# Order of the seven products of a feed-forward pair: the continuation of the first bank moves from third to fifth place

## What is computed

```python
h = rmsnorm(x, norm_ffn_pre[i])
gate, up = jnp.split(h @ ffn_w_gate_up[i], 2, axis=-1)
x = x + rmsnorm((jax.nn.silu(gate) * up) @ ffn_w_down[i], norm_ffn_post[i])
```

## Time and profile before

| | us |
|---|---|
| median of 3 runs | 3061.6 |
| lowest and highest | 3060.26, 3063.1 |
| profiled execution, its own time | 3064.46 |
| its span, first to last instruction | 3062.6 |
| the 20 pairs in it, first to last product | 705.9 to 950.3 |

### The profile page before, as it was taken

How to read it: one execution, slowest core, us unless ns; L and a number is a source line. 1 busy time by engine, 2 the same in 40 slices (tenths; PEclk the granted TensorE clock), 3 DMA queues, 4 the chain that set the end, 5 groups by cost and what they waited for, 6 DMA issues and landing times. The chain is left out here.

```text
span 3062.6 us, 43424 instructions
## 1 busy us (share of the span) xinstructions
PE 2715.5 (89%) x16618; PEld 1653.0 (54%) x16619; DVE 1141.4 (37%) x2326; ACT 654.9 (21%) x1327; POOL 312.2 (10%) x389
## 2 busy tenths in 40 slices
PE   7999999999999998999977999989788993898755
PEld 3445556578885484557554545445544642454323
DVE  2430157437889932227152111011422624232114
ACT  3440148421100010108131000000221621010002
POOL 0000012004441000000001100000100001122100
PEclk9999989999999999999988999999899996899887
DMA  5223120119545641120027889999632015999994
GB/s 201 83 83 101 53 97 29 59 56 259 198 161 199 259 181 59 55 90 1 28 75 296 346 352 412 397 413 382 256 126 89 1 63 204 370 364 377 404 418 170
DMA packets 137313, 594.52 MB, mean 194 GB/s; under 512 B 20336, under 2 KB 40588, under 8 KB 90608
## 3 DMA queue, kind: packets, MB, share of 16 engines
q1 hardware_dynamic: 86704, 359.25, 31.0%
q10 hardware_dynamic: 41808, 212.75, 17.3%
q0 software_dynamic: 8688, 21.00, 1.9%
HBM read 574.06 MB, written 33.69 MB: 198 GB/s over the span
## 5 line engine op out<-in xcount | busy, mean ns | idle before, releaser
L159 PE MATMUL psum<-normed,weight_ring 128*128 128x512 f32 (+1 forms) x896 | 365.2, 568 | 12.3 <-PEq L174 7.6
L159 PEld LDWEIGHTS psum<-normed,weight_ring 128*128 128x128 f32 x896 | 171.6, 192 | 201.4 <-issue 198.2
L1203 DVE SCALAR_TENSOR_TENSOR psum<-weight_ring,condition_rows 128x1024 f32<-128x1024 f32 x192 | 267.7, 1394 | 16.0 <-issue 0.9
L159 PE MATMUL psum<-modulated,weight_ring 128*128 128x384 f32 (+2 forms) x640 | 228.7, 518 | 0.0
L2469 PE MATMUL psum<-weight_ring,slot_rows_turned 128*32 128x256 f32 x2176 | 143.5, 409 | 73.3 <-DMA weight_ring<-in_w_dram 46.8
L2622 DVE COPY expert_hidden_turned<-psum 128x128 f32<-128x128 f32 (+1 forms) x93 | 32.7, 352 | 466.9 <-PE psum L2480 466.9
L2458 PE MATMUL psum<-weight_ring,slot_rows_turned 128*64 128x256 f32 x1792 | 205.3, 382 | 0.6 <-issue 0.6
L159 PEld LDWEIGHTS psum<-modulated,weight_ring 128*128 128x128 f32 x640 | 121.4, 190 | 105.5 <-issue 51.0
L2458 PEld LDWEIGHTS psum<-weight_ring,slot_rows_turned 128*64 128x64 f32 x1792 | 127.5, 138 | 76.0 <-issue 16.8
L2487 PE MATMUL psum<-weight_ring,expert_hidden_turned 128*32 128x256 f32 (+1 forms) x1536 | 168.0, 445 | 0.0
L2550 ACT ACTIVATE expert_silu<-psum 64x256 f32<-64x256 f32 (+1 forms) x91 | 34.6, 380 | 604.6 <-PE psum L2458 322.6
(11 more groups left out here) (444 smaller groups left out, 3791.7 us busy)
## 6 DMA issues: line engine op xcount, KB each, us to landing
third_stream_weights<-in_w_dram ACTq DMA_DIRECT2D x93, 2048.0 KB, 14.2
weight_ring<-in_w_dram SPq DMA_DIRECT2D x84, 2048.0 KB, 17.1
weight_ring<-in_w_ada_dram SPq DMA_DIRECT2D x24, 2048.0 KB, 8.9
weight_ring<-in_w_ffn_dram SPq DMA_DIRECT2D x11, 2048.0 KB, 12.8
weight_ring<-in_w_rnn_dram SPq DMA_DIRECT2D x8, 1536.0 KB, 11.8
weight_ring<-in_w_att_dram SPq DMA_DIRECT2D x6, 2048.0 KB, 8.0
weight_ring<-in_w_in_dram SPq DMA_DIRECT2D x6, 2048.0 KB, 12.8
weight_ring<-in_w_down_dram SPq DMA_DIRECT2D x8, 1408.0 KB, 6.4
```

The source lines that it names most:

```text
L159: last = nc.tensor.matmul(out, weights[:, k * P:(k + 1) * P], rhs(k), start=(k == 0), stop=(k == tiles - 1))
L1203: last = v.scalar_tensor_tensor(out=product, in0=w[:, t], scalar=1.0, in1=CR[:, n, :], op0=ALU.mult, op1=ALU.mult, accum_out=c.mod[:, i // ...
```

## The change

The product FIRST, with the wait on `first_copied` ahead of it, is issued two places later, behind SEVENTH and FIFTH; the table of places in the count follows. No instruction is added or removed, and the code of the other engines is the same; what each waits for is counted by the new table.

```diff
-        COPIED, SIXTH, FIRST, SEVENTH, FIFTH, FOURTH, LAST = range(1, 8)
+        COPIED, SIXTH, SEVENTH, FIFTH, FIRST, FOURTH, LAST = range(1, 8)
...
                     product(BANK6, in_slot(S2(p)), T2)
-                    first_copied.wait(pe, p + 1)
-                    product(BANK1(p), quarter(0, 1), B21, starts=False)
                     if p == 0:
                         token_sums.wait(pe, 4)
                     weight_sums.wait(pe, 4 * p + 3)
...
                     product(BANK5, in_slot(S1(p)), T1, stops=False)
+                    first_copied.wait(pe, p + 1)
+                    product(BANK1(p), quarter(0, 1), B21, starts=False)
                     product(BANK4, quarter(1, 1), T4)
```

## The result

The changed kernel is slower: median 3075.7 us (3069.04 to 3077.86, 5 runs) against 3060.44 (3060.0 to 3063.1, 5 runs) of the kernel before, ratio 1.0044, 95% interval 1.0029 to 1.0059. The interval stands for 9 to 18 us; the forecast was 11.8. Run again on the chip of the first experiments it had 3075.1 against 3062.61, ratio 1.0038 (1.0025 to 1.0052).

A forecast was written before the change was run, and what follows sets the result against it. VectorE's way from L1244 to L1239, then LAST, was taken to bound the long pairs. L1065 delaying an L1203 costs 14 x 0.84 = +11.8 us, so 3061.6 becomes 3073.4 us, range 3066 to 3079.

The forecast's parts named there:

- What bounds the long pairs: VectorE's work from L1244 to L1239, then LAST, was claimed to set their length, 12.24 us before the change.
- long pairs: Pairs whose predecessor is no multiple of 5: 2 to 19 without 6, 11 and 16; forecast 12.24 to 13.08 us.
- the 14 waits: TensorE's weight loads waiting for VectorE's L1239 ahead of LAST: 4.3 us in all, said to cost 2.1 us.
- The wait on the copy costs nothing: Ahead of FIRST: the copy ends at 744.65, FIRST starts at 745.80, so moving the wait gains 0.
- L1065 at 6.95 us after L1244: GpSimd's S4 starts earlier behind FIFTH, under one L1203, and lengthens the next from 1.23 to 2.07 us.
- 14 pairs, +11.8 us: The sum: 0.84 us later LAST in each of 14 pairs, giving +11.8 us.
- The short pairs: Pairs with one step of the other job less, as pair 1: 12.09 us, claimed cost of the change 0.
- The full block by the Trainium skill: Blocked L1203 runs its whole 1.23 us after GpSimd ends: 0.98 us a pair, 13.7 us, 3075.3 us.
- Later stages shift whole: Stages behind the pairs start from their end and should move by the full +11.8 us.
- L1239 did not wait for FIFTH: Rival that FIFTH holds `diagonal`, so its earlier place ends the waits: minus 2.1 us, 3059.5; chance 0.04.
- the clock stayed at 1.00: Rival that longer TensorE waits before LAST lower the clock: 59 us more, 3121 us; chance 0.02.
- no difference: Rival: GpSimd takes its turn after both L1203, or a later stage gives 11.8 us back: 3061.6; chance 0.10.

The follow-up runs named there:

- e5: Kernel before, old product order, one of the two L1203 steps ahead of L1236 moved behind L1239: 3061.33 us, ratio 0.9994.
- e6: Changed kernel, new product order, one of the two L1203 steps ahead of L1236 moved behind L1239: 3061.45 us, ratio 0.9991 against before.
- e3: Kernel before with only SEVENTH third and FIRST fourth, FIFTH staying fifth: 3063.16 us, ratio 1.0002.
- e0: The changed kernel run once more without edit: 3075.1 us against 3062.61 of the kernel before, ratio 1.0038.
- e7: e6 with the two L1203 steps behind the last pair done behind pairs 5 and 10 instead: 3054.22 us, ratio 0.9969 against before.
- e2: Kernel before with only FIFTH fourth and SEVENTH fifth, FIRST staying third: 3077.09 us, ratio 1.0048.
- e1: Changed kernel with GpSimd's L1065 waiting one product longer, for the fifth product as before: 3063.63 us, ratio 1.0004 against before.

## Why the prediction was right

*What bounds the long pairs.* VectorE's own way to L1239: confirmed by e5 and e6, which shorten it by one L1203: e6 brings all pairs to 12.09 us, and TensorE takes the same 241.5 us over the 20 in both. The prediction put the price of the 14 waits at 2.1 us, 0.15 each; it was 2.4, since pair 15 took 12.57 us before and not 12.24. There VectorE stood idle for 0.43 us ahead of L1236, for which the trace names no releaser. Nothing else in the forecast hangs on this.

*The wait on the copy costs nothing.* Right: e3 moves FIRST behind SEVENTH, for 232.03 us against 232.07.

*L1065 at 6.95 us after L1244, ending 1.12 us after the L1203 under which it starts.* Measured 6.95 and 1.11. The forecast length of the L1203 behind it was 2.07 us, measured 2.07 to 2.08; the long pair 13.08, measured 13.06 to 13.09 (13.41 in pair 15, which was 12.57 before).

*14 pairs, +11.8 us.* 14 waits, +11.7 us in the stage. The short pairs stay at 12.09; there L1065 starts at 7.13 us, under the second L1203, and ends 1.12 us behind it (pair 1: 725.19 and 724.07 us). It comes behind that L1203, as forecast, and no longer holds it up.

*The full block by the Trainium skill* (SBUF — State Buffer, section "Who interferes with whom"). The trace agrees with the page that the later one waits for the end of the other. The page gives no length for what is left after that; the whole 1.23 us was the prediction's own reading of it. A blocked L1203 ends 1.10 us after the block, and the stage's 11.7 us stand with the row's 11.8 and not with 13.7.

*Later stages shift whole.* Right for e0 (from the last L1244: 2112.6 us against 2112.3). In the first profile of the change it was off by 4.9 us, and 2.2 more ahead of the pairs. The forecast had allowed 3.4, for one fall of the clock; that was too little, and the clock alone does not explain the stretch shown above. The medians' +15.3 and +12.5 us lie above 11.8, but both intervals hold it. So the stage confirms the size closely; the total confirms only that it is of this order.

The rivals failed each where the prediction said: L1239 did not wait for FIFTH in long pairs, GpSimd was let in between the two L1203, and the clock stayed at 1.00 in the stretch in spite of 14 waits of 1.13 us (1.5 the longest). For the second half of *no difference*, that a later stage gives the time back, the first profile alone looked like a case, with 7.1 of the 11.7 us; e0 shows that it was not.

## What to carry to other kernels

VectorE and GpSimd instructions that both read two operands from SBUF take turns in all these runs: the one that came later, L1203 or L1065, ended about 1.1 us after the end of the other. So a semaphore count that starts a GpSimd instruction 1.7 us earlier can lengthen a VectorE instruction that was clear before, here from 1.23 to 2.08 us. Ask for each GpSimd instruction which VectorE instruction comes next and who waits for that. A busy engine need not be the bound: TensorE was at 50.00 of 50.00 us, and the round still went through VectorE. Side work that is spread into the gaps of another engine belongs behind the instruction that releases the main engine, not ahead of it: in e6 that ended the 14 waits, and with the two steps taken from behind the last pair as well (e7) the whole kernel was 6 to 12 us faster than before.

## What the runs showed of the hardware that was not expected

Executions of one program differ outside the pairs by more than the spread shown before the change had suggested: over the later runs before itself reached from 3058.53 to 3068.53 us, while the stage of the pairs repeated to 0.04 us (243.78, 243.82 and 243.79 in after, e0 and e2; 232.07, 232.06 and 232.03 in before, e1 and e3). For a change of this size the stage in one profile says more than the median of five totals.

The granted clock differed behind equal gaps. Behind the gap of 4.09 to 4.10 us ahead of the down projection it was 0.52 over 7 us in before and 0.76 in e6; behind the 1.74 us of e7 it stayed at 1.00, and so it did in the pairs of the changed kernel with 14 waits of 1.13 us.
